# Attention scores as products over 32 or 64 partitions instead of over zero-padded query blocks

## The chip, the cores and the metric

The kernel runs on one core of a Trainium2 chip. The metric is the device time of one execution in microseconds (us), as the median of several runs; lower is better.

## What is computed

One inference step of a streaming encoder, in fp32, for 1024 prompt tokens and 8 x 16 sample tokens (these with a cache of 256 keys each), width 1024. The layer's shape:

```python
a = rmsnorm(h)
[q_d|k_d|v_d|q_s|k_s|v_s] = a @ w_in
h += concat[diff_attn(q_d,k_d,v_d), stick_break(q_s,k_s,v_s)] @ w_out
h += PEER(rmsnorm(h))
h += (p @ w_ple) * sigmoid(rmsnorm(h) @ w_pgate)
y = rmsnorm(h)
```

Both kinds of attention have 8 heads of 64 elements. The differential one splits a head into two components of 32, each with scores of its own; the stick-breaking one takes the 64 whole:

```python
# diff_attn
s = einsum('bqhcd,bkhcd->bhcqk', qc, kc) * 32 ** -0.5      # c = 2 components of 32
s = where(k_pos // 64 <= q_pos // 64, s, -inf)
w = softmax(s)[:, :, 0] - lam * softmax(s)[:, :, 1]
# stick_break
z = einsum('bqhd,bkhd->bhqk', q, k) * 64 ** -0.5
log_keep = where(k_pos < q_pos, log_sigmoid(-z), 0)
wts = where(k_pos < q_pos, exp(log_sigmoid(z) + cumsum_of_later(log_keep)), 0)
```

PEER picks 16 of 16384 experts for each of 8 heads and each token. An expert is one row u (whose dot product with the token gives its weight after a gelu) and one row v (added with that weight), both of 1024 elements.

## The kernel before, in words

The first stage, `project_inputs`, makes queries, keys and values for 9 tiles of 128 tokens and writes queries and keys, transposed, to the DRAM tensor `qk_turned`, where a pair of heads (index m, 0 to 3) takes the 128 partitions: partitions 0 to 31 and 32 to 63 are the two components of the first head, 64 to 127 those of the second. For the stick-breaking kind partitions 0 to 63 are the first head's and 64 to 127 the second's.

The second stage, `attend_and_sum_experts`, is written by hand for all five engines at once, with semaphores. Its work is counted in steps of 16 expert rows per token. The 1024 prompt tokens form blocks i = 0 to 7 of 128 tokens. For each block there are four attending steps, one for each pair of heads m, numbered n = 4i + m; those of block i are done beside the expert rows of block i - 1, and those of block 0 (`attending_step(-1, m)`) before any expert row is gathered. After four attending steps come four steps in which block i goes through w_out and the choice of its experts, with expert rows of block i - 1 beside them. The samples' attention takes the place of the attending steps of a block 8. There are 72 steps with expert rows in all.

In an attending step each engine follows a fixed order:

- **SP** issues the loads. `load_keys(i, m)` waits until the scores of the step before have read their operands (`z_done`), and loads the keys of blocks 0 to i into `kd`, then the queries into `qd` (L530), later `ks` and `qs` the same way (L536, L538). `load_values` follows. Transfers of this kind are also behind the large loads of `w_out` and `w_query` at the stage's start.
- **PE** (`attention_scores`) makes six scores j: four for the components (j < 4, from `kd`) and two stick-breaking ones (from `ks`), each into one of two halves of `z_ps`. L809 is the product, in pieces of 512 keys; L811 adds the mask of the last 128 keys as the product of the identity with the mask. Between the scores stand `add_rows`, which add expert rows v into `sum_ps` (L789: a diagonal matrix of weights by the row), and after them `turn_weights` (L824) and `weigh_values` (L836). An fp32 matmul shows in the trace as two weight loads (PEld) and two passes (PE).
- **DVE** takes the maximum of each score (`maximum`, L1571), normalises, runs the stick-breaking scan, and between these makes the dot products with rows u (L1410) and adds a few rows v (L1424).
- **ACT** exponentiates the scores (L1150), makes the logarithms (L1158 to L1162), copies the turned weights (L1169) and makes the diagonals for PE (L1139).
- **POOL** gathers expert rows: one u row (L660) and one v row (L671) for each of 128 tokens a time, into rings of 4 and 8 buffers. A gather waits until DVE or PE has used the buffer it overwrites.

Before, a score product runs over all 128 partitions: `qd` has one block of 128 x 128 for each component j, in which only the 32 partitions of that component hold queries and the rest is zero; `qs` has two such blocks. POOL clears both once (L681, L682) and SP waits for it (`cleared`) ahead of its large loads; SP then writes only the 32 or 64 partitions of each block, in four transfers for `qd` and two for `qs`. The zeros stay for all steps. When the samples' turn comes, `s_stick` lies in `qd`.

Of the kernel before, what the change touches and what calls it, by code (L numbers as in the profile page):

```python
# [11 lines left out]
P = 128  # L12
# [216 lines left out]
KEYS = PAST + S  # L229
# [20 lines left out]
def attend_and_sum_experts(nc, const, ins, qk_turned, new_rows, heads, summed, y):  # L250
# [7 lines left out]
    with ExitStack() as ctx:  # L258
        def sb(name, shape, dt=F32):
            return ctx.enter_context(nc.sbuf_tensor(name, shape, dt))  # L260
# [4 lines left out]
        sem = stage_semaphores(nc, ctx)  # L265
# [28 lines left out]
        qd = sb("qd", [P, 4, P])  # L294
        qs = sb("qs", [P, 2, P])
# [10 lines left out]
        kd, ks, vd, vs = (place(n).rearrange("p (j k) -> p j k", k=P) for n in range(4))  # L306
# [35 lines left out]
        s_stick = qd[:, :, :].rearrange("p a n -> p (a n)")[:, 0:KEYS]  # L342
# [62 lines left out]
        cleared = sem("cleared")  # L405
        kd_in = sem("kd_in")
# [92 lines left out]
        def _(sp):  # L499
# [24 lines left out]
            def load_keys(i, m):  # L524
                n = 4 * i + m
                if n:
                    sp.wait_ge(z_done, 6 * n - 2)
                sp.dma_start(kd[:, 0:i + 1, :], qk_turned[1, m, :, 0:i + 1, :]).then_inc(kd_in, 16)
                for a in range(4):
                    sp.dma_start(qd[a * 32:(a + 1) * 32, a, :], qk_turned[0, m, a * 32:(a + 1) * 32, i, :]  # L530
                                 ).then_inc(kd_in, 16)
                if i and m == 0:
                    sp.wait_ge(query_turned, 4 * i)
                if n:
                    sp.wait_ge(z_done, 6 * n)
                sp.dma_start(ks[:, 0:i + 1, :], qk_turned[3, m, :, 0:i + 1, :]).then_inc(ks_in, 16)  # L536
                for a in range(2):
                    sp.dma_start(qs[a * 64:(a + 1) * 64, a, :], qk_turned[2, m, a * 64:(a + 1) * 64, i, :]  # L538
                                 ).then_inc(ks_in, 16)
# [35 lines left out]
            sp.wait_ge(cleared, 2)  # L575
# [70 lines left out]
        def _(pool):  # L646
# [34 lines left out]
            nc.gpsimd.memset(qd[:, :, :], 0.0).then_inc(cleared, 1)  # L681
            nc.gpsimd.memset(qs[:, :, :], 0.0).then_inc(cleared, 1)  # L682
# [34 lines left out]
        def _(pe):  # L717
# [76 lines left out]
            def attention_scores(i, j, n):  # L794
# [7 lines left out]
                if j == 0:  # L802
                    pe.wait_ge(kd_in, 80 * n + 80)
                if j == 4:
                    pe.wait_ge(ks_in, 48 * n + 48)
                q, kt, mask = (qd[:, j, :], kd, const.chunk_mask) if j < 4 else (qs[:, j - 4, :], ks, const.strict_mask)
# [1221 lines left out]
```

## Time and profile before

| | |
|---|---|
| median of 3 runs | 4390.84 us (4384.69 to 4396.41) |
| the profiled execution | 4385.67 us, its span 4384.0 us |
| busy in the span | PE 3443.2 us (79%), DVE 2834.4 (65%), POOL 2759.3 (63%), ACT 1181.7 (27%) |
| moved by DMA | 1355.99 MB, on average 309 GB/s |
| projections, span 0 to about 436 us | no expert rows yet |
| block 0's attention and choice of experts | about 436 to 636 us |
| expert rows, attention of blocks 1 to 7 beside them | about 636 to 3220 us |
| samples, then the last projection and the output | about 3220 to 4384 us |

The profile's engines are PE (matmul passes), PEld (weight loads, which overlap passes), DVE, ACT, POOL and SP. Lines such as L809 are lines of the kernel above. In the page, slices are tenths of busy time in 40 equal pieces of the span; a chain is what is found by following, from the last instruction back, what released each one. In a row of waits the numbers are the time waited, how often, and the longest. In a timeline a row gives start, length, engine, line, operands, and in brackets how long the engine had been idle and who ended that. The granted clock is TensorE's, as a share of 2.4 GHz; its two levels are 1.2 and 2.4 GHz, and a value between them is a mixture in time.

### The profile page before, as it was taken

The numbers are of one execution on the slowest core, as the hardware profiler recorded it, in microseconds if no ns is written. First come the engines' busy times: TensorE is split into PE (matmuls) and PEld (weight loads), VectorE is DVE, ScalarE is ACT, GpSimd is POOL, SyncE is SP. The second block draws the span as 40 slices with busy tenths as digits, with TensorE's granted clock in tenths as the row PEclk, the third lists the DMA queues.
The fourth block names the chain that finished last, engine by engine and source line by source line (L and its number), as shares of the span: only waits on it lengthen the run. The fifth ranks groups of instructions, "written<-read, shape, count | busy, mean of one in ns | idle before, by whom it ended". The sixth has DMA issues, their size and how long they took to land.

```text
span 4384.0 us, 33556 instructions
## 1 busy us (share of the span) xinstructions
PE 3443.2 (79%) x9668; PEld 1653.3 (38%) x9668; DVE 2834.4 (65%) x5497; ACT 1181.7 (27%) x2303; POOL 2759.3 (63%) x2364
## 2 busy tenths in 40 slices
PE   8998546877796787779687878877887777868877
PEld 3444323433342343344244334433442333323333
DVE  1121266686768768776876787687778554587775
ACT  0100314213312421441154135313531332111111
POOL 0000017777777777787777777777677544667875
PEclk9999678998899999999999998999999898989998
DMA  4111319999999999999999999999999887899996
GB/s 170 60 53 58 142 58 379 369 349 368 391 337 364 370 357 356 372 353 347 362 361 351 333 350 347 348 352 358 347 354 353 309 283 270 325 367 377 369 377 226
DMA packets 448998, 1355.99 MB, mean 309 GB/s; under 512 B 47296, under 2 KB 117824, under 8 KB 447808
## 3 DMA queue, kind: packets, MB, share of 16 engines
q0 software_dynamic: 333072, 1212.83, 74.4%
q1 hardware_dynamic: 115760, 141.21, 9.3%
q8 instruction: 73, 1.20, 0.1%
q14 instruction: 93, 0.76, 0.0%
HBM read 1325.54 MB, written 28.31 MB: 309 GB/s over the span
## 4 chain that ended last, share of the span: by engine, by line
PE 31%; POOL 24%; DMA 13%; issue 10%; DVE 9%; ACT 4%; SPq 0%; ACTq 0%; POOLq 0%; DVEq 0%
PE sum_ps L789 15%; POOL v_rows L671 12%; POOL u_rows L660 11%; PE z_ps L732 8%; DMA v_rows<-expert_v_in,idx_tile 6%; DMA u_rows<-expert_u_in,idx_tile 6%; DVE u_rows L1410 2%; PE z_ps L809 1%; DVE neg_max L1571 1%; PE z_ps L919 1%; DVE arena L1501 1%; PE out_ps L836 1%; ACT diag L1139 1%; PE z_ps L892 1%; DMA qd<-qk_turned 1%
## 5 line engine op out<-in xcount | busy, mean ns | idle before, releaser
L789 PE MATMUL sum_ps<-v_rows,diag 128*128 128x512 f32 x3460 | 1840.0, 669 | 619.2 <-DMA v_rows<-expert_v_in,idx_tile 396.3
L1410 DVE CUSTOM_DVE_ANT_0 u_rows<-u_rows,c_rows 128x1024 f32<-128x1024 f32 x1152 | 1405.2, 1225 | 624.5 <-DMA u_rows<-expert_u_in,idx_tile 608.7
L660 POOL DMA_INDIRECT u_rows<-expert_u_in,idx_tile x1152 | 1369.1, 1188 | 646.2 <-issue 313.2
L671 POOL DMA_INDIRECT v_rows<-expert_v_in,idx_tile x1152 | 1337.1, 1161 | 351.3 <-issue 317.8
L789 PEld LDWEIGHTS sum_ps<-v_rows,diag 128*128 128x128 f32 x3460 | 669.8, 209 | 1517.2 <-issue 853.0
L1139 ACT ACTIVATE diag<-ident,coef 128x128 f32<-128x128 f32 x865 | 312.8, 394 | 636.1 <-PE sum_ps L789 571.7
L142 PE MATMUL proj_ps<-weights,aT 128*128 128x512 f32 x864 | 378.5, 596 | 9.9 <-ACT aT L171 9.9
L1424 DVE SCALAR_TENSOR_TENSOR acc<-v_rows,coef,acc 128x1024 f32<-128x1024 f32 x278 | 357.3, 1285 | 10.7 <-DMA v_rows<-expert_v_in,idx_tile 10.6
L732 PE MATMUL z_ps<-w_query_sb,arena 128*128 128x512 f32 x576 | 255.4, 597 | 1.1 <-ACT arena L1101 1.1
L142 PEld LDWEIGHTS proj_ps<-weights,aT 128*128 128x128 f32 x864 | 162.9, 191 | 207.3 <-issue 195.1
L125 POOL TENSOR_TENSOR stat<-stat,minus_half 128x1 f32<-128x1 f32 x9 | 5.0, 557 | 338.5 <-DVE stat L193 338.5
L1150 ACT ACTIVATE arena<-z_ps,neg_max 128x128 f32<-128x128 f32 (+7 forms) x128 | 94.9, 741 | 451.8 <-DVE neg_max L1571 451.8
L1571 DVE TENSOR_REDUCE neg_max<-z_ps 128x1 f32<-128x128 f32 (+7 forms) x128 | 96.6, 754 | 173.5 <-PE z_ps L811 173.3
L809 PE MATMUL z_ps<-arena,qd 128*128 128x512 f32 (+3 forms) x384 | 154.2, 513 | 68.5 <-ACT arena L1150 49.6
L836 PEld LDWEIGHTS out_ps<-arena 128*128 128x128 f32 x1152 | 162.2, 208 | 99.5 <-issue 78.0
L824 PE MATMUL group_ps<-ident,arena 128*128 128x128 f32 x576 | 105.9, 295 | 107.5 <-ACT arena L1169 90.1
L836 PE MATMUL out_ps<-arena 128*128 128x64 f32 x1152 | 157.9, 286 | 32.6 <-ACT arena L1169 32.6
L732 PEld LDWEIGHTS z_ps<-w_query_sb,arena 128*128 128x128 f32 x576 | 108.9, 192 | 131.6 <-issue 128.1
L205 DVE TENSOR_TENSOR rot<-proj_ps,rope_tab 128x512 f32<-128x512 f32 x18 | 12.4, 691 | 213.6 <-PE proj_ps L142 213.6
L1501 DVE FIND_INDEX8 arena<-arena 128x8 uint32<-128x128 f32 (+1 forms) x432 | 134.3, 328 | 0.0
L824 PEld LDWEIGHTS group_ps<-ident,arena 128*128 128x128 f32 x576 | 71.6, 153 | 158.9 <-ACT arena L1169 105.6
L1169 ACT COPY arena<-group_ps 128x512 f32<-128x512 f32 (+3 forms) x192 | 90.5, 471 | 150.0 <-PE group_ps L824 149.9
(176 smaller groups left out, 3120.2 us busy)
## 6 DMA issues: line engine op xcount, KB each, us to landing
u_rows<-expert_u_in,idx_tile POOLq DMA_INDIRECT x1152, 6.5
v_rows<-expert_v_in,idx_tile POOLq DMA_INDIRECT x1152, 6.5
weights<-w_in_in SPq DMA_DIRECT2D x6, 2048.0 KB, 19.8
qk_turned<-turned SPq DMA_DIRECT2D x36, 256.0 KB, 2.8
w_out_sb<-w_out_in SPq DMA_DIRECT2D x2, 4096.0 KB, 18.7
w_query_sb<-w_query_in SPq DMA_DIRECT2D x1, 8192.0 KB, 28.7
x<-x_all_in POOLq DMA_DIRECT2D x9, 512.0 KB, 3.7
arena<-x_all_in SPq DMA_DIRECT2D x9, 512.0 KB, 7.1
```

The source lines that it names most:

```text
L142: mm = nc.tensor.matmul(proj_ps[:, g % 3, :], aT[:, k, :], weights[:, k, g * W:(g + 1) * W], start=(k == 0), stop=(k == KC - 1))
L660: pool.indirect_dma_start(u_rows[r % U_RING][:, :], None, ins["expert_u"], bass.IndirectOffsetOnAxis(ap=idx_tile[:, e % 2, at:at + 1], axis=0)
L671: pool.indirect_dma_start(v_rows[g % V_RING][:, :], None, ins["expert_v"], bass.IndirectOffsetOnAxis(ap=idx_tile[:, e % 2, at:at + 1], axis=0)
L732: mm = nc.tensor.matmul(acc_ps[:, bank, :], inT[:, k, :], weights[:, k, half * W:(half + 1) * W], start=(k == 0), stop=(k == KC - 1))
L789: mm = nc.tensor.matmul(sum_ps[:, half * W:(half + 1) * W], diag[:, by_tensor[g] % DIAGS, :], v_rows[g % V_RING][:, half * W:(half + 1) * ...
L809: nc.tensor.matmul(z_ps[:, j % 2, a:a + w], q, kt.rearrange("p j k -> p (j k)")[:, a:a + w], start=True, stop=a + w < width)
L824: mm = nc.tensor.transpose(group_ps[:, (k - a) * P:(k - a + 1) * P], src[:, k * P:(k + 1) * P], const.ident)
L836: mm = nc.tensor.matmul(out_ps[:, 64 * h:64 * h + 64], wT[:, k * P:(k + 1) * P], v[:, k, 64 * (h % 2):64 * (h % 2) + 64], start=(k == 0), ...
L1139: nc.scalar.mul(diag[:, j % DIAGS, :], const.ident, coef[:, (step - 1) % 2, g % TOP:g % TOP + 1]).then_inc(diag_done, 1)
L1410: nc.vector.tensor_tensor_reduce(row, row, c_rows[e % 2][:, :], 1.0, 0.0, ALU.mult, ALU.add, dots[:, s % 2, r % TOP:r % TOP + 1]).then_inc ...
L1424: nc.vector.scalar_tensor_tensor(acc[:, :], row, weight, acc[:, :], ALU.mult, ALU.add).then_inc(v_added, 1)
L1501: last = nc.vector.max_index(found[:, m, 8 * half:8 * half + 8], vals[:, m, 8 * half:8 * half + 8], src[:, m, :])
```

## The change

Queries are loaded as they are, 128 partitions by 128 tokens, by one transfer for `qd` and one for `qs`. Each score product takes the slice of partitions of its component (32) or head (64) from both operands. The mask product, all waits and the order on PE, DVE and ACT stay. The padding, POOL's two memsets and the semaphore `cleared` go; `s_stick` gets a buffer of its own.

```diff
--- before.py
+++ after.py
@@ -291,8 +291,9 @@
         sub_gain = sb("sub_gain", [P, 64])
         steps16 = sb("steps16", [P, TOP])
         mix = sb("mix", [P, D])
-        qd = sb("qd", [P, 4, P])
-        qs = sb("qs", [P, 2, P])
+        qd = sb("qd", [P, P])
+        qs = sb("qs", [P, P])
+        s_stick = sb("s_stick", [P, KEYS])[:, :]
         neg_max = sb("neg_max", [P, 4])
         total = sb("total", [P, 4])
         share = sb("share", [P, 4])
@@ -339,7 +340,6 @@
         fold = lent[:, 7 * D + W + 96:7 * D + W + 112]
         late_mask = lent[:, 7 * D + W + 112:7 * D + W + 128]
         s_soft = lent[:, 7 * D + W + 128:7 * D + W + 128 + KEYS]
-        s_stick = qd[:, :, :].rearrange("p a n -> p (a n)")[:, 0:KEYS]
         s_qT, s_newT = (place(n).rearrange("p (a c n) -> p a c n", a=2, c=4) for n in range(2))
         taken_by_samples = place(2, 7 * D)
         kT = taken_by_samples[:, 0:8 * KEYS].rearrange("p (a c n) -> p a c n", a=2, c=4)
@@ -402,7 +402,6 @@
         diag_done = sem("diag_done")
         sum_done = sem("rsum_done")
         sum_stored = sem("sum_stored")
-        cleared = sem("cleared")
         kd_in = sem("kd_in")
         ks_in = sem("ks_in")
         vd_in = sem("vd_in")
@@ -526,17 +525,13 @@
                 if n:
                     sp.wait_ge(z_done, 6 * n - 2)
                 sp.dma_start(kd[:, 0:i + 1, :], qk_turned[1, m, :, 0:i + 1, :]).then_inc(kd_in, 16)
-                for a in range(4):
-                    sp.dma_start(qd[a * 32:(a + 1) * 32, a, :], qk_turned[0, m, a * 32:(a + 1) * 32, i, :]
-                                 ).then_inc(kd_in, 16)
+                sp.dma_start(qd[:, :], qk_turned[0, m, :, i, :]).then_inc(kd_in, 16)
                 if i and m == 0:
                     sp.wait_ge(query_turned, 4 * i)
                 if n:
                     sp.wait_ge(z_done, 6 * n)
                 sp.dma_start(ks[:, 0:i + 1, :], qk_turned[3, m, :, 0:i + 1, :]).then_inc(ks_in, 16)
-                for a in range(2):
-                    sp.dma_start(qs[a * 64:(a + 1) * 64, a, :], qk_turned[2, m, a * 64:(a + 1) * 64, i, :]
-                                 ).then_inc(ks_in, 16)
+                sp.dma_start(qs[:, :], qk_turned[2, m, :, i, :]).then_inc(ks_in, 16)
 
             def load_values(i, m):
                 n = 4 * i + m
@@ -572,7 +567,6 @@
                 sp.wait_ge(s_taken, 2 * b + 2)
                 sp.dma_start(heads[b * S:(b + 1) * S, :], s_out).then_inc(s_stored, 16)
 
-            sp.wait_ge(cleared, 2)
             load_w_out()
             for m in range(4):
                 load_keys(0, m)
@@ -678,8 +672,6 @@
                     if step:
                         gather_v(r - TOP)
 
-            nc.gpsimd.memset(qd[:, :, :], 0.0).then_inc(cleared, 1)
-            nc.gpsimd.memset(qs[:, :, :], 0.0).then_inc(cleared, 1)
             for n in range(2):
                 power(0, n)
             for e in range(TP):
@@ -800,10 +792,13 @@
                 else:
                     pe.wait_ge(prob_done, 4 * n + (j - 1))
                 if j == 0:
-                    pe.wait_ge(kd_in, 80 * n + 80)
+                    pe.wait_ge(kd_in, 32 * n + 32)
                 if j == 4:
-                    pe.wait_ge(ks_in, 48 * n + 48)
-                q, kt, mask = (qd[:, j, :], kd, const.chunk_mask) if j < 4 else (qs[:, j - 4, :], ks, const.strict_mask)
+                    pe.wait_ge(ks_in, 32 * n + 32)
+                if j < 4:
+                    q, kt, mask = qd[32 * j:32 * j + 32, :], kd[32 * j:32 * j + 32, :, :], const.chunk_mask
+                else:
+                    q, kt, mask = qs[64 * j - 256:64 * j - 192, :], ks[64 * j - 256:64 * j - 192, :, :], const.strict_mask
                 for a in range(0, width, W):
                     w = min(W, width - a)
                     nc.tensor.matmul(z_ps[:, j % 2, a:a + w], q, kt.rearrange("p j k -> p (j k)")[:, a:a + w],
```

Of the order of instructions, two places. First SP, the loads of the last block's second and third step (i = 7), before and then with the change:

```order
235 L528 DMA arena<-qk_turned 128x1024 [waits z_done]
236 L530 DMA qd<-qk_turned 32x128 x4
237 L536 DMA arena<-qk_turned 128x1024 [waits z_done]
238 L538 DMA qs<-qk_turned 64x128 x2
239 L548 DMA arena<-new_dv 128x8x128 [waits out_done]
240 L548 DMA arena<-new_sv 128x8x128 [waits out_done]
```

```order
235 L527 DMA arena<-qk_turned 128x1024 [waits z_done]
236 L528 DMA qd<-qk_turned 128x128
237 L533 DMA arena<-qk_turned 128x1024 [waits z_done]
238 L534 DMA qs<-qk_turned 128x128
239 L543 DMA arena<-new_dv 128x8x128 [waits out_done]
240 L543 DMA arena<-new_sv 128x8x128 [waits out_done]
```

Six query transfers have become two; places and waits are the same. Then PE, the first scores of a step of block 4 (640 keys, so a piece of 512 and one of 128), with the change; the shapes are those of the outputs, and `arena` is where `kd` lies:

```order
1352 L804 MATMUL z_ps<-arena,qd 128x512 [waits kd_in,expo_done]
1353 L804 MATMUL z_ps<-arena,qd 128x128
1354 L806 MATMUL z_ps<-chunk_mask,ident 128x128
1355 L804 MATMUL z_ps<-arena,qd 128x512 [waits expo_done]
1356 L804 MATMUL z_ps<-arena,qd 128x128
1357 L806 MATMUL z_ps<-chunk_mask,ident 128x128
```

These rows differ from those before only in their line numbers (L804 and L806 were L809 and L811): nothing moved on PE, and a mask product over all 128 partitions still follows every score product.

## Rows read from the trace of the kernel before

**Rows 1.** The page: engines, slices of DMA, DMA queues, chain.

```profile
PE 3443.2 (79%) x9668; PEld 1653.3 (38%) x9668; DVE 2834.4 (65%) x5497; ACT 1181.7 (27%) x2303; POOL 2759.3 (63%) x2364
...
DMA  4111319999999999999999999999999887899996
...
q0 software_dynamic: 333072, 1212.83, 74.4%
q1 hardware_dynamic: 115760, 141.21, 9.3%
...
PE 31%; POOL 24%; DMA 13%; issue 10%; DVE 9%; ACT 4%; SPq 0%; ACTq 0%; POOLq 0%; DVEq 0%
```

**Rows 2.** Windows: busy of PE, PEld, DVE, ACT, POOL; clock, DMA share, GB/s.

```profile
1003.50:1190.00 186.50, 144.14 (x438) 74.64 (x437) 134.02 (x218) 80.66 (x162) 147.19 (x130) 0.91 1.00 381
...
2994.30:3218.00 223.70, 185.52 (x712) 105.96 (x711) 174.90 (x223) 116.12 (x175) 158.86 (x131) 0.93 0.95 344
```

**Rows 3.** Waits, stretches of i = 2, 5, 7: us, times, longest.

```profile
DVE u_rows L1410 <- DMA u_rows<-expert_u_in,idx_tile: 45.6, 38, 3.5
...
DVE u_rows L1410 <- DMA u_rows<-expert_u_in,idx_tile: 34.9, 26, 3.0
DVE neg_max L1571 <- PE z_ps L811: 14.4, 6, 4.1
...
DVE neg_max L1571 <- PE z_ps L811: 35.3, 8, 6.0
DVE u_rows L1410 <- DMA u_rows<-expert_u_in,idx_tile: 7.8, 6, 2.1
```

**Rows 4.** Chain by line: step at i = 3, step and stretch at i = 7.

```profile
by line: DMA u_rows<-expert_u_in,idx_tile 39.0%; DMA v_rows<-expert_v_in,idx_tile 14.0%; POOL v_rows L671 13.7%; issue 10.7%; POOL u_rows L660 9.3%; PE sum_ps L789 4.2%; DVE u_rows L1410 3.5%; DVE arena L1597 2.6%; DVE acc L1424 2.5%; DVE a
...
by line: PE sum_ps L789 35.4%; PE z_ps L809 16.3%; PE out_ps L836 11.9%; PE group_ps L824 8.0%; issue 6.2%; ACT arena L1169 5.1%; DVE neg_max L1571 4.2%; ACT L1160 2.3%; ACT arena L1162 2.0%; DVE u_rows L1410 2.0%; PE z_ps L811 2.0%; ACT ar
...
by line: PE sum_ps L789 25.4%; issue 7.9%; PE z_ps L809 7.7%; PE out_ps L836 7.2%; DVE neg_max L1571 6.9%; PE group_ps L824 6.2%; DVE u_rows L1410 4.3%; DMA v_rows<-expert_v_in,idx_tile 4.3%; DMA u_rows<-expert_u_in,idx_tile 4.1%; ACT arena
```

**Rows 5.** Block 0, second step: window; PE's timeline at its start.

```profile
474.60:490.70 16.10, 9.43 (x37) 7.64 (x37) 4.72 (x16) 10.46 (x25) 0.00 (x0) 0.61 0.07 20
...
474.65 0.77 PE L809 MATMUL z_ps<-arena,qd 128*128 128x128 f32 x2 [6.54 <-DMA qd<-qk_turned]
```

**Rows 6.** Timeline of PE at i = 7: start, length, instruction, count.

```profile
3120.40 1.88 PE L809 MATMUL z_ps<-arena,qd 128*128 128x512 f32 x4
...
3122.34 1.88 PE L809 MATMUL z_ps<-arena,qd 128*128 128x512 f32 x4
```

**Rows 7.** L919: matmuls of two sizes (min/median/max ns); then PEld's timeline.

```profile
L919 PE MATMUL z_ps<-w_out_sb,arena x3: 587/592/692, 3483.9 to 3485.0; 16*128 16x512 f32 x2, 128*128 128x512 f32 x1
...
3496.85 0.19 PEld L919 LDWEIGHTS z_ps<-w_out_sb,arena 128*128 128x128 f32 x1 [0.24 <-issue]
3497.28 0.19 PEld L919 LDWEIGHTS z_ps<-w_out_sb,arena 128*128 128x128 f32 x1 [0.24 <-issue]
3498.23 0.29 PEld L919 LDWEIGHTS z_ps<-w_out_sb,arena 16*128 16x128 f32 x2 [0.76 <-issue]
3499.28 0.30 PEld L789 LDWEIGHTS sum_ps<-v_rows,diag 128*128 128x128 f32 x2 [0.76 <-issue]
3499.81 0.19 PEld L789 LDWEIGHTS sum_ps<-v_rows,diag 128*128 128x128 f32 x1 [0.24 <-issue]
```

**Rows 8.** Waits for L530; timeline of POOL and SP at the stage's start.

```profile
  PE z_ps L809: 18.1, 2
...
436.54 0.31 POOL L682 MEMSET qs<- 128x256 f32 x1
...
437.43 0.47 SPq L510 DMA_DIRECT2D w_out_sb<-w_out_in  x1
...
438.57 1.92 SPq L530 DMA_DIRECT2D qd<-qk_turned  x4
```

**Rows 9.** Windows of L809 alone, i = 4 to 7, their sum.

```profile
sum 848.10, PE 150.44 PEld 69.06; mean PE 37.61 PEld 17.27
```

## The prediction

> **What bounds the kernel now.** I read the views from coarse to fine. First the page: PE is busy 79% of the span, the DMA engines stand at nine tenths in nearly every slice from the seventh on, and no single engine carries the chain that ended last: PE has 31% of it, POOL 24%, DMA 13% [rows 1]. Such a mean hides stages, so next I cut the span at the blocks i of the prompt. An attending stretch (four attending steps, the only place where the changed products run) lasts 186.5 us at i = 2 and 223.7 us at i = 7, while the DMA share falls from 1.00 to 0.95 and PE's busy time grows from 144 to 186 us [rows 2]. Then the waits of the same stretches. At i = 2 DVE waits 45.6 us for gathered u rows, so the gathers are late and PE is not. At i = 7 that wait is 7.8 us, DVE waits 35.3 us for score products on PE instead, and then the gathers, which wait for DVE's dots, come late [rows 3]. The chains say the same: in a step at i = 3 it is made of gathers, with 4.2% of PE; in a step at i = 7 the PE lines alone make up 74% of it [rows 4]. So **the early blocks (i = 1 to 3) are bound by the gathers, the late ones (i = 6, 7) mostly by PE**, 4 and 5 lie between, and block 0, where no gather runs yet, is a serial chain of PE, DVE and ACT at a granted clock of 0.61, near the lower of its two levels, 1.2 GHz [rows 5].
>
> **The products themselves.** A score is one product per 512 keys, each executed as two passes; 32 steps by 6 scores are 192 scores. In a dense stretch at 2.4 GHz four passes of 512 columns and the two of the mask (0.22 us) follow each other without a gap: 3120.40 to 3122.34 us [rows 6]. Fewer rows of the array do not shorten a pass. The trace has a matmul with few rows already: the third product of L919 uses 16 partitions. The two passes of one take 587 and 692 ns (the longer has its weight load inside), the full-row pass ahead of them 592 [rows 7], so I cost the smaller products at **zero saving**.
>
> **What the same matmul shows is the price.** Look at the weight loads around it [rows 7]. Among full-row products they start every 0.43 us (3496.85, 3497.28). From 3497.28 to 3499.81 five further loads start (two each at 3498.23 and 3499.28, one at 3499.81), which would take 5 x 0.4285 = 2.14 us, by the spacing of passes in [rows 6], (3122.34 - 3120.40 less the mask's 0.22) / 4, and take 2.53. The 0.39 us too many lie at its two edges, where PEld is idle 0.76 us instead of 0.24: going from 128 rows to few costs about **0.195 us** and coming back costs the same. After the changed rows a load waits until the array has emptied. All 16 such products stand the same way; one of them is in the rows. This agrees with the Trainium skill, "TensorEngine Tiling (Array Packing)", Key Properties, that changing the tiling mode drains the engine; the page gives no time.
>
> Every changed score goes 128 to 32 (or 64) rows for its product and back to 128 for the mask product behind it, since the order on PE stays as it is. So 2 x 192 = 384 changes of mode, 12 in each attending step: 12 x 0.195 = 2.35 us of PE time a step, 75 us in all. What of it reaches the end, block by block:
> - **Block 0.** The first step is covered: PE then waits 6.54 us for the next queries, which queue behind w_query [rows 5], and 12 changes fit into that. In the other three the chain runs through all six scores one after the other; the first entry finds PE idle, so I count 10. At 1.2 GHz no row shows a change of mode. Bounds are the 0.195 above and twice that; I take 0.3, because the pass behind the change doubles and the wait for the array need not. 3 x 10 x 0.3 = 9 us, bounds 5 to 14.
> - **Blocks 1 to 3.** 12 x 2.35 = 28 us, under gathers that are late anyway (DVE's 45.6 us of waiting [rows 3]). A late score can delay a max, the dot behind it on DVE and so a gather, but seldom. I take 15%: 4 us, bounds 0 and 28. If this cover were gone, all 28 would show.
> - **Blocks 4 and 5.** 8 x 2.35 = 19 us. DVE still waits 34.9 us for u rows at i = 5, but also 14.4 us for scores [rows 3]. I take 35%: 6.6 us, bounds 2 and 19.
> - **Blocks 6 and 7.** 19 us. Queued behind the longer PE work are the max of the next score on DVE, the dots behind that, and by them POOL's gathers. The chain over the whole stretch of i = 7 still has shares of gathers beside PE's [rows 4], so not all counts: 75%, 14 us, bounds 9 and 19.
>
> **What is taken away.** Six query transfers a step become two with the same bytes. PE waited for queries only twice, 18.1 us, both in block 0 [rows 8] and both behind the large w_out and w_query loads, whose bytes stay; their landing is hidden otherwise. On SP the issues shrink from about 1.9 us for four to one [rows 8]; SP waits for PE between steps, so nothing starts earlier that is waited for. On the DMA engines each transfer ends in about 16 small packets: of the gather queue's 333072 packets the 2304 gathers of 128 rows leave 38160 [rows 1]. 128 transfers fewer are then some 2,000 packets; at the SP queue's mean, 9.3% of 16 x 4384 us over 115760 packets = 56 ns, they are worth at most 7 us of the 16 engines together. These packets are its smallest, and half the steps are not bound there: I take 1.5 us. The two memsets on POOL end at 436.85 us and the first transfer that waited for them is issued at 437.43, right behind the one before it [rows 8], so the wait cost nothing and its going gives nothing. POOL next waits for DVE in any case. The stick weights of the samples in a buffer of their own change no wait. A rule would price the transfers otherwise. The Trainium skill, "DMA: Bandwidth & Descriptors", Anatomy of one DMA, puts about 2.0 us of fixed cost on each transfer; by it, taken serially, 128 fewer would save an estimated 256 us. It speaks of latency, which the rows show overlapped, and I give such a saving less than 0.01; the sum goes by the rows.
>
> **Sum:** 9 + 4.2 + 6.6 + 14 - 1.5 = +32 us. Against the profiled execution, 4385.7 us (span 4384.0), that is 4418; the median of the runs shown, 4390.8, lies 5.2 us above the profiled one, and on that scale I forecast **4423 us**.
>
> **Rivals.**
> - *Hidden.* The slack of the late blocks takes the changes too (the granted clock of 0.93 and PE busy 186 of 224 us leave 38 us of gaps at i = 7 [rows 2]) and only block 0 shows: +9 - 1.5, 4398 us. Against it: the gaps are waits for ACT inside PE's own chain. Chance 0.13.
> - *No price.* Products of 32 and 64 rows might change over without the empty stretch that those of 16 have: -1.5, 4389 us. The edges were equal each time I looked. 0.05.
> - *Faster: row groups overlap.* The Trainium skill, "TensorE: Matmul & The Clock Gate", in its section on why this matters, says that products on distinct groups of 32 partitions run at the same time. As a mechanism here: score 1 stands behind score 0 with only the mask between [rows 6]; if its passes ran beside score 0's, a step of blocks 4 to 7 would save up to four passes of 0.43 us, 16 x 1.7 = 27 us, while those of 1 to 3 stay under the gathers: 4362 us. It decides if passes of another row group start before the mask pass has ended. Against it: the mask product needs all rows and stands between every two, and matmuls in the trace start in order. 0.03.
> - *All exposed.* The 75 us plus another 5 for the lower clock of block 0: 4471 us. It would need late scores to starve the gathers in the early blocks too. 0.05.
> - *The clock falls.* If few busy rows let the granted clock drop to 1.2 GHz in the score products, those of blocks 4 to 7 (150 us busy [rows 9]) take twice as long, mostly in the open: about +120 with the forecast's 32, 4543 us. Around the 16-row products the loads keep their 0.43 us spacing, so 2.4 GHz held, but those are short. 0.04.
>
> **Numbers.** The forecast has 0.70. Its own bounds, added, give 5 + 0 + 2 + 9 - 7 = +9 to 14 + 28 + 19 + 19 = +80; both ends together are unlikely. A range of 4398 to 4460 holds it nearly whole and the hidden case; outside are no price, overlap, all exposed and the clock, 0.17. About 0.3% (13 us) is what a measurement can tell from no change: below 4378 counts as faster (0.03), above 4404 as slower (0.70 + 0.05 + 0.04 = 0.79), between them the hidden case and the one without a price (0.18).
>
> **What would show it.** Right: L804 matmuls of 32 and 64 rows with PEld idle 0.7 us or more at each edge instead of 0.24; a score with its mask at i = 7 about 2.33 us from start to start instead of 1.94; late attending steps longer by some 2 us with the granted clock at 0.9; DVE waiting longer for z_ps; blocks 1 to 3 within 2 us of before per stretch; the second start of block 0 unmoved. Wrong: edges at 0.24; starts of score 1 before the mask's end; a granted clock under 0.85 in the late stretches; or attending stretches of i = 2 and 3 longer by 9 us like the late ones.

## The result and the profile after

The changed kernel takes **4420.0 us** (median of 9 runs), the kernel before 4387.2 us (9 runs): ratio 1.0082, interval 1.0065 to 1.0100, so 36 us slower by the ratio (28 to 44), 33 us by the medians. The forecast was +32 us, 4423 us, with a range of 4398 to 4460. The profiled execution took 4408.4 us, span 4406.7, and differs from the profiled one before by only 22.7 us. Single executions of one kernel scatter by some 10 us, so I take sizes from all executions and places from the profiles. In what follows a size in us is what the ratio has over 1, times the time before; sizes by the medians differ from it by up to 5 us.

The page after, the lines that answer to [rows 1]:

```profile
PE 3523.9 (80%) x9668; PEld 1645.8 (37%) x9668; DVE 2833.9 (64%) x5497; ACT 1183.2 (27%) x2303; POOL 2752.1 (62%) x2362
...
PEclk9999567999898899999999999998899888998998
...
q1 hardware_dynamic: 113712, 141.20, 9.2%
...
PE 35%; POOL 21%; DMA 11%; DVE 10%; issue 9%; ACT 4%; SPq 0%; ACTq 0%; POOLq 0%; DVEq 0%
```

PE is busy 81 us longer with the same 9668 matmuls, and has 35% of the chain instead of 31%. The SP queue (q1) has lost 2048 packets and no bytes, 16 for each of the 128 transfers. No other engine's busy time moved by more than 8 us.

Next the attending stretches of i = 2 and i = 7, cut at the same matmuls as [rows 2] (columns as there), after:

```profile
1013.70:1198.50 184.80, 153.58 (x437) 72.92 (x436) 133.12 (x217) 80.94 (x163) 142.14 (x131) 0.88 1.01 386
3000.80:3237.00 236.20, 201.71 (x711) 106.39 (x711) 175.48 (x223) 116.08 (x175) 159.37 (x131) 0.88 0.92 326
```

At i = 2 PE is busy 9.4 us longer and the stretch is 1.7 us shorter: the gathers still set its length. The waits of DVE show how: at i = 2 it now waits 15.4 us for scores instead of 5.6, and for u rows 34.2 us instead of 45.6, about the same sum. At i = 7 PE is busy 16.2 us longer and the stretch is 12.5 us longer. The mean granted clock of the two stretches is 0.88 and 0.88 instead of 0.91 and 0.93, which the forecast's sum did not have. The waits of DVE at i = 7, after:

```profile
DVE neg_max L1566 <- PE z_ps L806: 43.5, 10, 7.1
DVE u_rows L1405 <- DMA u_rows<-expert_u_in,idx_tile: 7.2, 6, 2.2
```

DVE waits 43.5 us for scores instead of 35.3 [rows 3]; over the whole kernel that wait has grown from 173.3 to 217.5 us.

The price itself, seen on two scores of i = 7. First PE, then PEld, after; start, length, instruction, count and idle time before it:

```profile
3063.14 1.98 PE L804 MATMUL z_ps<-arena,qd 32*128 32x512 f32 x4
3065.05 0.49 PE L806 MATMUL z_ps<-chunk_mask,ident 128*128 128x128 f32 x2
3065.47 2.17 PE L804 MATMUL z_ps<-arena,qd 32*128 32x512 f32 x4
3067.58 0.80 PE L806 MATMUL z_ps<-chunk_mask,ident 128*128 128x128 f32 x2
```

```profile
3064.11 0.18 PEld L804 LDWEIGHTS z_ps<-arena,qd 32*128 32x128 f32 x1 [0.24 <-issue]
3065.05 0.30 PEld L806 LDWEIGHTS z_ps<-chunk_mask,ident 128*128 128x128 f32 x2 [0.76 <-issue]
...
3067.57 0.50 PEld L806 LDWEIGHTS z_ps<-chunk_mask,ident 128*128 128x128 f32 x2 [0.95 <-issue]
```

The first score with its mask takes 3065.47 - 3063.14 = **2.33 us** where it took 1.94 [rows 6]: two changes of 0.195 us, exactly as costed, with the 0.76 us of idle loader at the edge. The second shows something else. Its product and mask stretch to 3068.16, 2.69 us, and the loader's gap is 0.95 us: the granted clock is 1.00 up to 3067 us and 0.56 in the microsecond behind, so it fell to its lower level, 1.2 GHz. PE had last waited at 3059.11 us, for 0.73 us, and had been busy without a break since.

Last, block 0, where the forecast had no row for a change at 1.2 GHz. PE from the start of the second step, after:

```profile
472.77 0.76 PE L804 MATMUL z_ps<-arena,qd 32*128 32x128 f32 x2 [3.98 <-DMA qd<-qk_turned]
473.46 0.80 PE L806 MATMUL z_ps<-chunk_mask,ident 128*128 128x128 f32 x2
474.19 0.79 PE L804 MATMUL z_ps<-arena,qd 32*128 32x128 f32 x2
...
479.97 0.79 PE L804 MATMUL z_ps<-arena,qs 64*128 64x128 f32 x2
...
481.28 0.42 PE L819 MATMUL group_ps<-ident,arena 128*128 128x128 f32 x1
```

and the same places before:

```profile
475.64 0.63 PE L809 MATMUL z_ps<-arena,qd 128*128 128x128 f32 x2
476.07 0.63 PE L811 MATMUL z_ps<-chunk_mask,ident 128*128 128x128 f32 x2
...
480.69 0.34 PE L824 MATMUL group_ps<-ident,arena 128*128 128x128 f32 x1
```

Before, the two passes of a 128-column product took 476.07 - 475.64 = 0.43 us, so the four of score and mask 0.85; now a score starts (479.97 - 472.77) / 5 = 1.44 us after the last. That is 0.29 us for each change at 1.2 GHz, against the forecast's 0.3. The price is the same for 32 rows (from `qd`) and for 64 (from `qs`). The step as a whole grows by less than its changes: from the first score to the first `group_ps` product it takes 8.51 us instead of 6.04 (its start before, 474.65, is in [rows 5]), +2.5, since some scores had waited a little before.

### The profile page after: what moved, and what is told of

The parts are those of the page before. It is cut to its first block, busy times and chain, and to the rows that moved or that the text cites. A ratio compares the mean times of both kernels' runs of the same rounds, so it can differ in the third digit from the quotient of the medians.

```text
span 4406.7 us, 33426 instructions
## 1 busy us (share of the span) xinstructions
PE 3523.9 (80%) x9668; PEld 1645.8 (37%) x9668; DVE 2833.9 (64%) x5497; ACT 1183.2 (27%) x2303; POOL 2752.1 (62%) x2362
## 4 chain that ended last, share of the span: by engine, by line
PE 35%; POOL 21%; DMA 11%; DVE 10%; issue 9%; ACT 4%; SPq 0%; ACTq 0%; POOLq 0%; DVEq 0%
PE sum_ps L781 16%; POOL u_rows L654 10%; POOL v_rows L665 10%; PE z_ps L724 8%; DMA v_rows<-expert_v_in,idx_tile 5%; DMA u_rows<-expert_u_in,idx_tile 4%; DVE u_rows L1405 3%; PE z_ps L804 3%; PE out_ps L831 1%; DVE arena L1496 1%; PE z_ps L806 1%; PE z_ps L914 1%; PE group_ps L819 1%; DVE neg_max L1566 1%; DVE arena L1536 1%
## 5 line engine op out<-in xcount | busy, mean ns | idle before, releaser
L1566 DVE TENSOR_REDUCE neg_max<-z_ps 128x1 f32<-128x128 f32 (+7 forms) x128 | 96.7, 755 | 217.7 <-PE z_ps L806 217.5
L804 PE MATMUL z_ps<-arena,qd 32*128 32x512 f32 (+3 forms) x384 | 170.3, 552 | 64.6 <-ACT arena L1145 49.1
L645 POOL TENSOR_TENSOR rstat<-rstat,minus_half 128x8 f32<-128x8 f32 (+1 forms) x18 | 29.5, 1642 | 228.0 <-DVE rstat L1451 176.0
```

The costliest lines, as they stand in the source:

```text
L804: nc.tensor.matmul(z_ps[:, j % 2, a:a + w], q, kt.rearrange("p j k -> p (j k)")[:, a:a + w], start=True, stop=a + w < width)
```

## The experiments

A change of mode is a step of PE from a product over 128 rows to one over 32 or 64, or back. Theory A is the forecast's: these changes are the whole loss. Its rivals are the other part of the change (the transfers and memsets) and B, that products over few rows cost something besides their edges. All edits but one are made to the kernel before; unless a diff shows more, they stand in `attention_scores`, behind the line that sets `q, kt, mask`. The clock given with a run is the mean granted clock over all its executions, with its standard error.

### 1. The slices alone, and the transfers alone

`e1_sliced_only` keeps padded blocks, transfers and memsets and slices the operands only:

```diff
                 q, kt, mask = (qd[:, j, :], kd, const.chunk_mask) if j < 4 else (qs[:, j - 4, :], ks, const.strict_mask)
+                if True:
+                    at = slice(32 * j, 32 * j + 32) if j < 4 else slice(64 * j - 256, 64 * j - 192)
+                    q, kt = (qd[at, j, :], kd[at, :, :]) if j < 4 else (qs[at, j - 4, :], ks[at, :, :])
```

> The kernel before with its zero-padded query blocks and all its transfers and memsets; only the products take the 32 or 64 partitions that hold queries. Same 384 changes of mode as the change. Theory (changes of mode cost the time, the transfers nothing): the whole loss appears here, ratio to before 1.0075 (+33 us), edges of 0.76 us idle on PEld. Rival (fewer or differently issued transfers slow the start or the loads): ratio near 1.000.

`e2_packed_full` is the changed kernel with its products over all 128 partitions. It leaves out the separation of heads and components, so it does not compute what is asked and stands here for its time alone:

```diff
-                if j < 4:
-                    q, kt, mask = qd[32 * j:32 * j + 32, :], kd[32 * j:32 * j + 32, :, :], const.chunk_mask
-                else:
-                    q, kt, mask = qs[64 * j - 256:64 * j - 192, :], ks[64 * j - 256:64 * j - 192, :, :], const.strict_mask
+                q, kt, mask = (qd[:, :], kd, const.chunk_mask) if j < 4 else (qs[:, :], ks, const.strict_mask)
```

> The changed kernel's packed queries, two transfers a step and no memsets, but products over all 128 partitions (each score is then the sum over all components of a pair of heads, which is not what the reference asks). No change of mode. Theory: ratio 1.000, at most 1.5 us faster than before. Rival (the transfers carry the loss): ratio 1.0075. If the 2 us that the second step of block 0 started earlier in the changed kernel come from the transfers, they show here too.

Measured: e1 4425.3 us, ratio **1.0076** (1.0056 to 1.0095), e2 4384.6 us, ratio **0.9995** (0.9983 to 1.0007), before 4388.3. The slices carry the whole loss. All that went with the padding (128 transfers, two memsets, a wait) is worth 2 us with an interval that holds zero. The second step of block 0, which started 1.9 us earlier in the changed kernel, starts at 474.83 us in e2's trace and at 474.65 before, so the transfers did not move it. And the clock, which no expectation had named, tells the two runs apart: 0.9125 (± 0.0005) before, 0.9111 (± 0.0007) in e2, **0.8995 (± 0.0008) in e1**; the changed kernel has 0.9001 (± 0.0012). With two levels, 1 and 0.5 of 2.4 GHz, a mean of 0.9125 is 17.5% of the time at the lower one, 768 us, and 0.8995 is 20.1%, 889 us. So B has a candidate: 121 us more at the lower clock.

### 2. By block

The same slices under a condition: `e3_block0` in block 0, `e5_blocks1to5` in blocks 1 to 5, `e6_blocks6and7` in the last two. `e12_late_again` repeats e6 with a later set of runs, because e6 decides most.

```diff
+                if i == 0:
+                    at = slice(32 * j, 32 * j + 32) if j < 4 else slice(64 * j - 256, 64 * j - 192)
+                    q, kt = (qd[at, j, :], kd[at, :, :]) if j < 4 else (qs[at, j - 4, :], ks[at, :, :])
```

> Kernel before, products sliced in block 0 only, 48 changes of mode at 1.2 GHz. Theory: the 9 us forecast for this block, ratio 1.002, block 1's first scores 5 to 9 us later, nothing after that. Rival (the chain has slack there): 1.000.

> Kernel before, products sliced in blocks 1 to 5 only (20 of the 28 attending steps beside gathers). The forecast's shares (15% and 35% of 0.195 us a change) give +11 us, ratio 1.0025. Rival A (every attending step beside gathers costs the same): 20/28 of the 26 us that sliced products cost outside block 0, +19 us, 1.0042. Rival B (early blocks hidden wholly): below 1.001.

> Kernel before, products sliced in blocks 6 and 7 only (8 steps). The forecast's share of 75% gives +14 us, ratio 1.0032. Rival A (same cost in every step): 8/28 of 26 us, +7 us, 1.0017.

> The kernel of e6_blocks6and7 again (32 or 64 partitions in blocks 6 and 7), beside the two others of this group on the same chip. If 1.0061 (interval 1.0044 to 1.0077) was typical: 1.005 to 1.007, granted clock 0.907. If it was high by chance and the forecast's share is right: 1.003.

| slices in | median us | ratio | interval | clock | forecast |
|---|---|---|---|---|---|
| block 0 (e3) | 4396.8 | 1.0008 | 0.9996 to 1.0021 | 0.9088 ± 0.0009 | +9 |
| blocks 1 to 5 (e5) | 4402.0 | 1.0036 | 1.0021 to 1.0051 | 0.9063 ± 0.0009 | +11 |
| blocks 6, 7 (e6) | 4412.8 | 1.0061 | 1.0044 to 1.0077 | 0.9073 ± 0.0017 | +14 |
| blocks 6, 7 (e12) | 4411.1 | 1.0059 | 1.0038 to 1.0081 | 0.9070 ± 0.0007 | +14 |

In us the parts are 4 (-2 to 9), 16 (9 to 22) and 26 (19 to 34). The late blocks have nearly twice what the forecast gave them, more than either ratio named for e6 ahead of it; block 0 and blocks 1 to 5 are within their errors of the forecast. e5 does not decide between its theory (1.0025) and its rival A (1.0042): both lie in its interval. The parts sum to 46 with an error of some 11, the whole is 33 to 36 with 8: they need not add up exactly, and the difference is no finding.

### 3. Changes of mode without small products

If A is the whole story, changes alone must cost the same. `e7_tiny` leaves every product at 128 rows and puts a product of 4 columns over 32 partitions ahead of it. It changes mode as often as the changed kernel, 384 times, and its few rows are busy for almost no time. The full product then overwrites its output.

```diff
+                at = slice(32 * (j % 4), 32 * (j % 4) + 32)
+                nc.tensor.matmul(z_ps[:, j % 2, 0:4], (qd if j < 4 else qs)[at, j % 2, :], (kd if j < 4 else ks)[at, 0, 0:4],
+                                 start=True, stop=True, skip_group_check=True)
```

> Kernel before with all products over 128 partitions; ahead of each of them stands one product of 4 columns over 32 partitions, whose result the next one overwrites. So there are the same 384 changes of mode, but almost no pass over few rows; PE has some 0.1 us more to do per score for the extra passes. The mean granted clock is 0.9125 before and 0.900 with sliced products. Theory 1 (the changes of mode carry everything, the lower clock too): ratio 1.0075 to 1.010, granted clock 0.900. Theory 2 (the passes over few rows themselves lower the granted clock and part of the loss comes from that): granted clock stays at 0.91 and the ratio is 1.003 to 1.006.

`e8_rows64` has the same 384 changes, with 64 partitions for all six products (for the first four a pair of components, of which one is zero padding):

```diff
+                at = slice(64 * (j // 2), 64 * (j // 2) + 64) if j < 4 else slice(64 * j - 256, 64 * j - 192)
+                q, kt = (qd[at, j, :], kd[at, :, :]) if j < 4 else (qs[at, j - 4, :], ks[at, :, :])
```

> Kernel before, all products sliced to 64 partitions (a component's 32 with 32 zero ones beside them), 384 changes of mode as in the changed kernel, but twice the rows in four of the six scores. Theory 1 (changes of mode): ratio 1.0076 and granted clock 0.900 as with 32. Theory 2 (the fewer rows, the lower the clock): granted clock 0.904 to 0.908, ratio 1.004 to 1.006.

PE in the last block of e7:

```profile
3072.01 0.38 PE L808 MATMUL z_ps<-arena,qd 32*128 32x4 f32 x2
3072.32 1.98 PE L812 MATMUL z_ps<-arena,qd 128*128 128x512 f32 x4
3074.14 0.38 PE L814 MATMUL z_ps<-chunk_mask,ident 128*128 128x128 f32 x2
3074.45 0.38 PE L808 MATMUL z_ps<-arena,qd 32*128 32x4 f32 x2
```

A score takes 3074.45 - 3072.01 = 2.44 us: 0.50 more than before, of which 0.39 are the two changes and 0.11 the two tiny passes. Over 192 scores that is 96 us of PE time, more than the 75 us of the changed kernel. Yet e7 loses no more than e1: 4411.8 us, ratio **1.0057** (1.0037 to 1.0077). The intervals of the two overlap, so the times alone do not part them, but the clock does: **0.9138** (± 0.0007), not below before's. And e8: 4406.9 us, ratio **1.0037** (1.0022 to 1.0052), clock 0.9080 (± 0.0007). Between the edits of e8 and e1 nothing differs but the rows of four products of six, 64 or 32, and 0.0039 of 4388 is 17 us, with an error of some 11; the two were timed on different chips, each beside the kernel before.

So A holds, and is not all. Changes alone make the kernel slower. On top of them, the fewer rows the score products use the lower is the mean granted clock: 0.9125, 0.9080, 0.8995 for 128, 64 and 32 or 64 rows.

### 4. The late blocks again, three ways

The same comparison where most of the loss is: the tiny product of e7 (`e10_tiny_late`) and the 64 rows of e8 (`e11_rows64_late`), each only for i >= 6, beside e6 and e12.

```diff
+                if i >= 6:
...
```

> The tiny 32-row products of e7_tiny in blocks 6 and 7 only, 96 changes of mode, full products. PE gets 8 x 6 x 0.5 = 24 us more to do. Theory 1 (most of what e6_blocks6and7 lost, ratio 1.0061, is the time of the changes): 1.004 to 1.005. Theory 2 (most of it is the lower granted clock of the passes over few rows): 1.001 to 1.003, granted clock 0.913.

> Products over 64 partitions in blocks 6 and 7 only. Same changes as e6_blocks6and7. Theory 2: between e10_tiny_late and e12_late_again, about 1.003, granted clock 0.910. Theory 1: the same as e12_late_again.

| blocks 6 and 7 | ratio | interval | clock |
|---|---|---|---|
| changes alone (e10) | 1.0018 | 1.0003 to 1.0033 | 0.9135 ± 0.0008 |
| 64 rows (e11) | 1.0021 | 1.0004 to 1.0039 | 0.9136 ± 0.0009 |
| 32 and 64 rows (e12) | 1.0059 | 1.0038 to 1.0081 | 0.9070 ± 0.0007 |

The clock does not fall at all at 64 rows here, where 0.910 had been expected.

Do 32 rows cost more at their edges than 64? No. Here are the first two scores of the last step of i = 7 and the expert rows that follow them, of e11:

```profile
3171.41 1.98 PE L812 MATMUL z_ps<-arena,qd 64*128 64x512 f32 x4
...
3173.73 1.98 PE L812 MATMUL z_ps<-arena,qd 64*128 64x512 f32 x4
...
3179.07 5.37 PE L789 MATMUL sum_ps<-v_rows,diag 128*128 128x512 f32 x8 [2.93 <-ACT diag L1142]
```

and the same place of e12:

```profile
3179.76 2.00 PE L812 MATMUL z_ps<-arena,qd 32*128 32x512 f32 x4
...
3182.41 3.78 PE L812 MATMUL z_ps<-arena,qd 32*128 32x512 f32 x4
...
3189.85 6.35 PE L789 MATMUL sum_ps<-v_rows,diag 128*128 128x512 f32 x8 [2.94 <-ACT diag L1142]
```

At 2.4 GHz a score of 64 rows takes 3173.73 - 3171.41 = 2.32 us, as one of 32 does (2.33 above), so the edges cost the same. In e12 the clock falls at the end of the first product (its mean over this piece is 0.59, e11's is 1.00), and from the first score to the expert rows it takes 10.09 us instead of 7.66.

The windows 2570 to 3240 us, which hold both blocks' steps, of e11 and e12 (columns as in [rows 2]). First e11:

```profile
2570.00:3240.00 670.00, 551.42 (x1787) 273.67 (x1788) 506.39 (x827) 262.26 (x431) 496.78 (x408) 0.94 0.94 345
```

and e12:

```profile
2570.00:3240.00 670.00, 559.05 (x1751) 276.59 (x1751) 497.11 (x810) 258.27 (x422) 485.19 (x400) 0.90 0.92 338
```

This is the plainest pair of the study. Both have the same changes of mode in the same places, at the same price. At 64 rows the clock stays and the blocks lose 9 us, as the tiny products do with 8. At 32 rows the clock in the window is 0.90 instead of 0.94, PE is busy longer with 36 matmuls fewer done in the time, and the loss is 26 us. The 17 us between them (13 by the medians) go with the clock. One window of one profile would not prove it: the same window has 0.91 in e2, with full rows, and 0.92 in the changed kernel. The means over all executions carry it (0.9136 and 0.9070, and 0.9073 in e6), and PE's busy time over the whole kernel goes with them, 3459.3 us in e11's profile and 3475.5 in e12's.

The traces also show where the clock falls. The table counts the falls to 1.2 GHz between 600 and 3240 us, and how many of them came while PE had been busy for over 90% of the 6 us before. The 6 us are my choice for the count and say nothing of how the chip decides; 4 or 8 give the same picture.

| score products | traces | falls | with PE that busy |
|---|---|---|---|
| 128 rows | before, e2, e3 | 242 | 0 |
| 128 rows, tiny ones ahead | e7, e9, e10 | 205 | 1 |
| 64 rows | e8, e11 | 151 | 0 |
| 32 and 64 rows | after, e1, e5, e6, e12 | 392 | 51 |
| two of 32 side by side | e4 | 76 | 0 |

With full rows the clock fell only where PE had stood idle for part of the time. With lone 32-row products one fall in eight came in the middle of dense work, each of these five traces having at least six of them.

### 5. Twice the changes

`e9_tiny_twice` puts three tiny products (32, 128 and 32 rows) ahead of each: 768 changes.

```diff
+                for rows in (slice(32 * (j % 4), 32 * (j % 4) + 32), slice(0, P), slice(32 * (j % 4), 32 * (j % 4) + 32)):
+                    nc.tensor.matmul(z_ps[:, j % 2, 0:4], (qd if j < 4 else qs)[rows, j % 2, :],
+                                     (kd if j < 4 else ks)[rows, 0, 0:4], start=True, stop=True, skip_group_check=True)
```

> As e7_tiny, but ahead of each product stand three products of 4 columns, over 32, 128 and 32 partitions: 768 changes of mode instead of 384, all full products over 128 partitions. A score then holds about 0.50 us (e7) plus 0.39 us for two more changes plus up to 0.2 us for passes more than before. Theory (the changes cost their time on PE, and the slack is used up the more of them there are): ratio 1.013 to 1.018, granted clock 0.91 or above. Rival (e7's loss was something else about the small products, their count being what matters): 3 times e7's, 1.017; or nothing new, 1.006.

Measured: 4484.3 us, ratio **1.0228** (1.0203 to 1.0254), clock 0.9148 (± 0.0011). PE in the last block of e9:

```profile
3100.19 1.01 PE L808 MATMUL z_ps<-arena,qs 32*128 32x4 f32 x6
3101.13 1.99 PE L812 MATMUL z_ps<-arena,qs 128*128 128x512 f32 x4
3102.95 0.38 PE L814 MATMUL z_ps<-strict_mask,ident 128*128 128x128 f32 x2
3103.17 1.88 PE L789 MATMUL sum_ps<-v_rows,diag 128*128 128x512 f32 x4
```

A score takes 3103.17 - 3100.19 = 2.98 us, 1.04 more than before, twice the 0.50 of e7. The kernel loses four times as much: 25 us became 100. That is more than was expected by the theory (1.013 to 1.018) or by either rival. Of the first 96 us of PE time about a quarter reached the end, of the next 104 about 70% did. So most of the first part fitted into waits that PE's work did not set, little of the second did, and a share read from one size does not carry to twice that size. The clock stays where it was, so changes of mode do not lower it.

### 6. Row groups side by side

The faster rival needed two products of different row groups to stand next to each other; the mask product between them prevents that. `e4_pair` makes the place: in every step the first two scores are issued piece by piece in turn, over partitions 0 to 31 and 32 to 63 into different banks, and their masks follow. The other four stay as before.

```diff
+            def first_scores(i, n):
...
+                for a in range(0, width, W):
+                    w = min(W, width - a)
+                    for j in range(2):
+                        at = slice(32 * j, 32 * j + 32)
+                        nc.tensor.matmul(z_ps[:, j, a:a + w], qd[at, j, :],
+                                         kd[at, :, :].rearrange("p j k -> p (j k)")[:, a:a + w],
+                                         start=True, stop=a + w < width)
...
-                attention_scores(i, 0, n)
-                attention_scores(i, 1, n)
+                first_scores(i, n)
```

> Kernel before, but scores 0 and 1 of each step are made together: their pieces of 512 keys alternate between partitions 0 to 31 and 32 to 63 into different banks, then both masks; scores 2 to 5 padded as before. Two changes of mode a step. If products of different row groups overlap, the four passes pairs of a late step take half: first scores at i = 7 about 1.9 + 0.4 us instead of 3.9, and the kernel is 5 to 15 us faster than before (ratio 0.998). If they don't, they take 3.9 + 0.4 us and the ratio is 1.001.

PE in the last block of e4: the pair, the expert rows behind it and, of the same step, a score of 128 rows:

```profile
3180.48 1.99 PE L824 MATMUL z_ps<-arena,qd 32*128 32x512 f32 x8
3182.40 0.71 PE L828 MATMUL z_ps<-chunk_mask,ident 128*128 128x128 f32 x4
3188.10 5.73 PE L789 MATMUL sum_ps<-v_rows,diag 128*128 128x512 f32 x8 [4.99 <-ACT diag L1155]
3193.66 1.88 PE L809 MATMUL z_ps<-arena,qd 128*128 128x512 f32 x4
3195.38 0.39 PE L811 MATMUL z_ps<-chunk_mask,ident 128*128 128x128 f32 x2
```

Eight passes of 512 columns take 1.99 us, the time that four take. The passes of the two groups start 6 to 7 ns apart, and no change is paid between two products on different groups of 32 rows, only on entering and leaving. So the mechanism is real, in the two-pass form of this kernel too. The Trainium skill has it in "TensorE: Matmul & The Clock Gate", the section on why this matters, with starts at most 4 ns apart; here they are 6 to 7 ns.

The kernel was still **not faster**: 4398.1 us, ratio 1.0021 (1.0006 to 1.0036), with a clock of 0.9052 (± 0.0010). The trace shows why the faster pair gains nothing. Before, the same two scores and the expert rows behind them:

```profile
3162.44 1.94 PE L809 MATMUL z_ps<-arena,qd 128*128 128x512 f32 x4
...
3169.81 5.37 PE L789 MATMUL sum_ps<-v_rows,diag 128*128 128x512 f32 x8 [3.27 <-ACT diag L1139]
```

The two scores and their masks took PE from 3162.44 to 3166.53 us, 4.1 us, and now take 2.6 (3180.48 to 3183.11). But then PE waits for ACT, 4.99 us instead of 3.27, and from the first score to the expert rows it takes 3188.10 - 3180.48 = 7.62 us instead of 7.37, alike in three of the four steps of i = 7 (in the first it is 8.67 instead of 9.06). The chain behind it is DVE's first maximum, ACT's exponential, the same two for the second score, and then ACT's diagonal for the expert rows. DVE's first maximum starts 2.44 us after the first score starts (3182.92) where it started after 2.20 (3164.64), because with the pair the first mask stands behind all eight passes. Every piece behind it takes as long as before, so the whole chain comes 0.25 us later and the time that PE saves turns into waiting. How much the lower clock adds was not tried by itself, and why it is lower here stays open.

## Why the forecast was right, and where it was not

**The bound by stage: right.** The gathers hide 9 us of PE time at i = 2 completely; at i = 7 the stretch grows by 12.5 of the 16 us.

**No saving from fewer rows: right.** Four passes of 32 x 512 take the 1.72 us that those of 128 rows take: 3065.05 - 3063.14 = 1.91, less one change.

**0.195 us a change at 2.4 GHz, 0.3 at 1.2: right**, 2.33 us for a score in place of 1.94 and 0.29 us in block 0. The rival without a price falls. The price, read from one matmul of 16 rows that occurs 16 times, carried over to 32 and 64 rows as it was.

**Transfers and memsets, -1.5 us: right**, -2 us by e2's ratio (-7 to 3). Packets fell by 2048 as counted. No latency of the 128 transfers shows. The 2.0 us of fixed cost for each transfer, which the Trainium skill has in "DMA: Bandwidth & Descriptors", Anatomy of one DMA, is given there for transfers that POOL issues, while SP issues these; a cost of that size, if they have it, overlaps here, as the prediction took it.

**Block 0, +9 us: within the error.** +4 us (-2 to 9) in e3's runs, 8.5 by the medians. The traces place it better. From the second step's first score to the first score of block 1 it takes 119.99 us before (474.65 to 594.64), 127.53 in the changed kernel (472.77 to 600.30) and 127.50 in e3: +7.5 us. The three steps have 6.2 of these, at a granted clock of 0.50 where they had 0.61, and the products behind them the rest, at 0.83 where they had 0.86. The bounds of 5 to 14 do not follow from the 30 changes counted there, which at 0.195 and 0.39 us give 6 to 12. The second start did not move later, as named: the wait for queries took the first step's changes, 3.98 us of it being left of 6.54.

**Blocks 1 to 5, +11 us: the total holds, its reason only partly.** e5 has 16 us (9 to 22), with the clock down to 0.906, and that clock is not in the forecast. e7 less e10, changes alone in blocks 0 to 5, is 17 us, with an error of some 11, for 0.50 us of PE time a score where the slices cost 0.39.

**Blocks 6 and 7, +14 us: wrong, in two terms that partly cancel.** Measured: 26 us. The step that failed is the sum itself, which has no term for the clock, and that term is the larger part of the loss, about 17 us. The share of 75% also looks too high: of the 19 us of changes 9 reach the end in e11 (2 to 17, which still holds 14), and of the 24 us that the tiny products add in e10 8 do (1 to 14, where 75% would be 18).

**"The clock falls", 0.04: the mechanism is in the result, at a seventh of its size.** I priced it as all or nothing, 1.2 GHz in every score product of blocks 4 to 7, +120 us, and took as evidence against it that the clock held around a few short products of 16 rows. What happens is a shift in the share of time at the lower level, from 17.5% to about 20%. That some of it shows was to be bounded from below as well: a part of the 150 us of [rows 9] at the lower clock belonged into the sum with a chance of its own, not only the whole as a rival. The signs named in advance, 0.9 for right and under 0.85 for wrong in the late stretches, leave a gap, and the 0.88 measured lies in it.

**The sum, +32 against +33 to +36: a good total of less good parts.** By e8, 384 changes with larger products cost 16 us (10 to 23), some of it itself clock; the forecast gave the changes 34. About half of the loss is then changes of mode, about half goes with the granted clock. So the total came out right partly by luck: a share that was too high stood in for a term that was missing. The division is an estimate from e8 against e1 and e11 against e12: no run has 32-row products at an unchanged clock, so how it splits in blocks 0 to 5 stays open. The scatter within one kernel gives a check. Over the 185 executions of the experiments and the changed kernel, each taken against the mean of its own kernel and chip, a clock lower by 0.01 goes with 11 us (± 2) more. By that the 0.0130 of e1 is worth 14 us, near the 17; the 0.0066 of the late blocks would be 7, less than the 13 to 17 found there, where PE is what bounds.

**Hidden, all exposed.** Neither: the late blocks did not take it, and 75 us of PE time cost 36. e9 shows that it could have: with another 104 us of PE time 70% of them are exposed.

No version here beats the kernel before. e2 is the same within its interval, and it does not compute what is asked.

## What to carry to other kernels

Zero-padded operands that keep a product at 128 rows can be the cheaper form. Here passes took as long with 32 rows as with 128, a lone small product among full ones cost two changes of mode of 0.2 us each, and slicing to 32 rows lowered the granted clock besides. Use slices only where several products of one mode can follow each other, and then look whether the consumer wants the first result early: in e4 the saved time turned into waiting for it. When costing a change to PE's work, give the clock a term, and compare the granted clock over several runs, not in one profile. And before you apply a share to added PE time, ask how much of it the waits can still take.

## What the runs showed of the hardware that was not expected

- The granted clock depended on how many rows the products use, with the same columns and order: 0.9125 at 128 rows, 0.9080 at 64, 0.8995 at 32 and 64, the last two with the same changes of mode. Adding matmuls of 4 columns over 32 rows left it where it was (0.9138), even three to a score with a full one between (0.9148).
- In the late blocks alone 64 rows did not lower it (0.9136) and 32 did (0.9070); in e8, with 64 rows in all blocks, they do. Where is not settled: e8's profile has 0.92 both at 1000 to 1760 us and at 2570 to 3240 us, and the kernel before 0.93.
- With lone 32-row products the clock could fall in the middle of dense work, as at 3067 us, 8 us after PE's last wait: 51 of 392 falls, against 1 of 598 with 64 or 128 rows.
- A change of mode costs 0.195 us at 2.4 GHz and 0.29 at 1.2, one and a half times as much and not twice. Between two products of 32 rows on different partitions nothing is paid, and their passes run side by side.
